# Expert weights in 8 MB units with 16 KB runs and two places, instead of 4 MB units with 8 KB runs and three

## What is computed

```
h = rms_norm(x);  proj = h @ w_in            # q|k|v, RWKV-7 inputs, two gates
attn = sliding_window_attention(q, k, v);  y = rwkv7(...)
merged = sigmoid(ga) * (attn @ w_branch_a) + sigmoid(gb) * (y @ w_branch_b)
x = x + merged @ w_out                       # the output projection, 16 MB of weights
hf = rms_norm(x)
# router: best of 4 groups, best 2 of its 8 experts; for each of 32 experts e:
x[tok] += weight[tok, e] * ((silu(hf[tok] @ w_gate[e]) * (hf[tok] @ w_up[e])) @ w_down[e])
out = rms_norm(x) * final_norm_w
```

## Time and profile before

| | |
|---|---|
| three runs, lowest, median, highest | 1857.42, 1860.07, 1862.98 us |
| the profiled execution, its own time | 1861.89 us |
| its span in the profile | 1860.0 us |
| PE, DVE, ACT busy | 1454.8, 503.5, 347.7 us (78%, 27%, 19%) |
| DMA traffic | 529.04 MB, 284 GB/s over the span |
| chain that ended last | PE 57%, DMA 34%, DVE 4%, ACT 3% |
| mean granted clock of TensorE | 0.89 of full speed |

### The profile page before, as it was taken

How to read it: one execution, slowest core, us unless ns; L and a number is a source line. 1 busy time by engine, 2 the same in 40 slices (tenths; PEclk the granted TensorE clock), 3 DMA queues, 4 the chain that set the end, 5 groups by cost and what they waited for, 6 DMA issues and landing times.

```text
span 1860.0 us, 24062 instructions
## 1 busy us (share of the span) xinstructions
PE 1454.8 (78%) x10818; PEld 834.8 (45%) x10818; DVE 503.5 (27%) x666; ACT 347.7 (19%) x399; POOL 37.3 (2%) x33
## 2 busy tenths in 40 slices
PE   7999999999989999998767567575575665765754
PEld 7999964447546758886312113122121221211311
DVE  5555444252253256644101001010010100100102
ACT  5444332311121134444101001000010000100001
POOL 1000000002001100000000000000000000000000
PEclk9999999899979999999869779788887888977887
DMA  9555424240202239555699999999999999999993
GB/s 355 189 180 181 143 96 147 95 147 21 97 33 76 99 123 331 196 226 203 274 421 422 422 422 422 422 422 422 422 422 421 422 422 421 422 422 421 423 422 146
DMA packets 114524, 529.04 MB, mean 284 GB/s; under 512 B 7408, under 2 KB 9722, under 8 KB 64410
## 3 DMA queue, kind: packets, MB, share of 16 engines
q1 hardware_dynamic: 109616, 514.50, 69.2%
q0 software_dynamic: 2048, 8.24, 1.2%
q10 hardware_dynamic: 2794, 5.31, 0.8%
HBM read 521.74 MB, written 6.29 MB: 284 GB/s over the span
## 4 chain that ended last, share of the span: by engine, by line
PE 57%; DMA 34%; DVE 4%; ACT 3%; issue 1%; ACTq 0%; DVEq 0%; SPq 0%; POOL 0%; POOLq 0%
DMA ring<-in_expert_w_down 17%; DMA ring<-in_expert_w_up 11%; PE ps L508 11%; PE ps L571 10%; PE ps L843 9%; PE ps L961 7%; DMA ring<-in_expert_w_gate 6%; PE ps L978 5%; PE ps L987 3%; PE ps L930 2%; PE ps L470 1%; PE ps L734 1%; PE ps L751 1%; PE ps L553 1%; PE ps L753 1%
## 5 line engine op out<-in xcount | busy, mean ns | idle before, releaser
L961 PE MATMUL ps<-ring,arena 128*32 128x512 f32 x1280 | 184.7, 729 | 99.9 <-DMA ring<-in_expert_w_up 78.7
L571 PE MATMUL ps<-ring,arena 128*128 128x512 f32 x512 | 232.5, 607 | 3.2 <-ACT rs L1141 3.2
L978 PE MATMUL ps<-ring,arena 128*32 128x512 f32 x768 | 129.6, 836 | 85.6 <-DMA ring<-in_expert_w_down 83.5
L961 PE MATMUL ps<-arena 128*32 128x512 f32 x768 | 124.3, 807 | 76.5 <-DMA arena<-in_expert_w_up 46.2
L508 PE MATMUL ps<-h_hi,w_hi 128*128 128x256 f32 x544 | 155.2, 285 | 4.3 <-DVE w_lo L1399 4.3
L508 PE MATMUL ps<-h_lo,w_hi 128*128 128x256 f32 x544 | 155.0, 285 | 0.0
L508 PE MATMUL ps<-h_hi,w_lo 128*128 128x256 f32 x544 | 154.9, 285 | 0.0
L571 PEld LDWEIGHTS ps<-ring,arena 128*128 128x128 f32 x512 | 96.5, 194 | 118.6 <-issue 111.0
L961 PEld LDWEIGHTS ps<-ring,arena 128*32 128x32 f32 x1280 | 47.1, 130 | 223.5 <-issue 128.7
L1799 DVE TENSOR_TENSOR arena<-arena,ps 128x512 f32<-128x512 f32 x64 | 44.0, 688 | 345.1 <-PE ps L987 345.1
L978 PEld LDWEIGHTS ps<-ring,arena 128*32 128x32 f32 x768 | 31.0, 146 | 178.6 <-DMA ring<-in_expert_w_down 87.9
(11 more groups left out here) (292 smaller groups left out, 1798.7 us busy)
## 6 DMA issues: line engine op xcount, KB each, us to landing
ring<-in_expert_w_up SPq DMA_DIRECT2D x24, 4096.0 KB, 25.5
ring<-in_expert_w_down SPq DMA_DIRECT2D x24, 4096.0 KB, 23.9
ring<-in_w_in SPq DMA_DIRECT2D x34, 2048.0 KB, 8.2
arena<-in_expert_w_gate SPq DMA_DIRECT2D x16, 4096.0 KB, 23.7
ring<-in_expert_w_gate SPq DMA_DIRECT2D x16, 4096.0 KB, 23.7
arena<-in_expert_w_up SPq DMA_DIRECT2D x8, 4096.0 KB, 16.5
arena<-in_expert_w_down SPq DMA_DIRECT2D x8, 4096.0 KB, 23.4
ring<-in_w_out SPq DMA_DIRECT2D x8, 2048.0 KB, 7.9
```

Source lines behind the costliest of these rows:

```text
L571: last = mm(ps[:, 7, :], hT[:, k, 128 * t:128 * t + 128], slot(n)[:, k % 8, :], start=k == 0, stop=k == KT - 1)
L961: last = mm(ps[32 * j:32 * j + 32, u % 2, :], XS[:, k, 32 * j:32 * j + 32], w[:, j, kk, :], start=k == 0, stop=k == KT - 1, tile_position= ...
L978: last = mm(ps[32 * j:32 * j + 32, 2 + nb, :], HIDT[:, kh, 32 * j:32 * j + 32], w[:, j, 512 * nb:512 * nb + 512], start=kh == 0, stop=kh == 3,
```

## The change

- A unit is 8 MB: eight blocks of input rows of gate or up for four experts, so that a partition reads 16 KB in one run. A group is six units (gate, up, gate, up, down, down). The down matrices are read with the rows of a partition adjacent, unit 4 in 16 KB runs; unit 5 comes in two parts with runs of 8 KB, each with its own semaphore. The hidden values are transposed with a step of four columns to match.
- There are two places of 8 MB instead of three of 4 MB: even units in arena 0 to 8191 and ring slots 2 and 3, odd units in ring slots 0 and 1 and arena 12288 to 20479. A unit is loaded when the unit two before it is used, in two DMAs of 4 MB (unit 5: four of 2 MB).
- w_out uses ring slots 0 and 1 only: chunk c waits for chunk c-2. Behind the chunks 2 to 5 SyncE issues one quarter (2 MB) each of unit 0. The first half of unit 1 follows when all chunks are used, its second half when TensorE has done its last piece (`v_used` at UM + UO).
- `hfn` moves to arena 8192, over `hfT`, and so ScalarE waits for the logits (`lgT_ps`) before it writes it. `XS`, `YS` and the small tiles move to arena 25344 and up.
- `FW` lies over `XS` now, and GpSimd loads it when unit 3 of the last group is used.
- `gather(3)` runs right behind `gather(2)`, both after unit 0. The second path is adapted; it is left out here.

```diff
--- before.py
+++ after.py
@@ -222,24 +222,25 @@
...
-        hfn = A(12288, 4096).rearrange("p (a d) -> p a d", a=TT)
+        hfn = A(8192, 4096).rearrange("p (a d) -> p a d", a=TT)
         fout = hfn
         hfT = A(8192, 4096).rearrange("p (k t) -> p k t", k=KT)
...
-        junk2 = A(16384, 4096).rearrange("p (a d) -> p a d", a=TT)
+        junk2 = A(12288, 4096).rearrange("p (a d) -> p a d", a=TT)
-        XS = A(16384, 2048).rearrange("p (k s) -> p k s", k=KT)
-        YS = A(18432, 2048)
...
-        FW = A(27648, 2048)
+        XS = A(25344, 2048).rearrange("p (k s) -> p k s", k=KT)
+        YS = A(27392, 2048)
...
+        FW = A(25344, 2048)
@@ -294,7 +295,9 @@

         def v_piece(x):

-            return x // 4, ring[:, x // 4 % RING, 1024 * (x % 4):1024 * (x % 4) + 1024]
+            c = x // 4
+            s = c % RING if x < UM else c % 2
+            return s, ring[:, s, 1024 * (x % 4):1024 * (x % 4) + 1024]
@@ -307,15 +310,22 @@
-        UPG = 12
-        ROWS = 4
-
-        def uslot(u):
-
-            s = u % 3
-            if s == 0:
-                return A(0, 2 * SLOT), S("unit_full0")
-            return ring[:, 2 * s - 2:2 * s, :].rearrange("p a n -> p (a n)"), S(f"unit_full{s}")
+        UPG = 6
+        ROWS = 8
+
+        def place(u, j):
+
+            if u % 2:
+                return ring[:, j, :] if j < 2 else A(12288 + SLOT * (j - 2), SLOT)
+            return A(SLOT * j, SLOT) if j < 2 else ring[:, j, :]
+
+        def pair(u, h):
+
+            if u % 2 == h:
+                first = A(12288 if h else 0, 2 * SLOT)
+                return first.rearrange("p (j n) -> p j n", j=2)
+            return ring[:, 2 * h:2 * h + 2, :]
+
         assert NM % RING == 0 and NO % RING == 0
...
@@ -368,37 +378,54 @@
                     for o, n, key in ((0, 4, "router_group_w"), (4, 32, "router_expert_w")):
                         sp.dma_start(rw[:, :, o:o + n], a[key][0].rearrange("(k p) n -> p k n", p=P)).then_inc(S("rw_in"), 16)
             wo = a["w_out"][0].rearrange("(k p) n -> p k n", p=P)
-            for c in range(8):
-                load(NO + c, slot(NO + c), wo[:, 8 * (c % 2):8 * (c % 2) + 8, 512 * (c // 2):512 * (c // 2) + 512])
-
             eg = a["expert_w_gate"][0].rearrange("e (p k) h -> p e (k h)", p=P)
             eu = a["expert_w_up"][0].rearrange("e (p k) h -> p e (k h)", p=P)
-            ed = a["expert_w_down"][0].rearrange("e (k p) n -> p e k n", p=P)
-
-            def uload(u, first):
-
-                dst, full = uslot(u)
-                if u < 8:
-                    src = (eu if u % 2 else eg)[:, bass.ds(first, GE), ROWS * HID * (u // 2):ROWS * HID * (u // 2 + 1)]
+            ed = a["expert_w_down"][0].rearrange("e (p k) n -> p e (k n)", p=P)
+
+            for c in range(8):
+                sp.wait_ge(S("chunk_used"), NM + 5 + c if c < 2 else NO + c - 1)
+                sp.dma_start(ring[:, c % 2, :].rearrange("p (k n) -> p k n", k=8),
+                             wo[:, 8 * (c % 2):8 * (c % 2) + 8, 512 * (c // 2):512 * (c // 2) + 512])\
+                    .then_inc(S(f"slot_full{c % 2}"), 16)
+                if 2 <= c < 6:
+
+                    if c == 2:
+                        sp.wait_ge(S("v_used"), UM)
+                    if c == 4:
+                        sp.wait_ge(S("chunk_used"), NO)
+                    sp.dma_start(place(0, c - 2), eg[:, c - 2, 0:SLOT]).then_inc(S("unit_full0"), 16)
+
+            def half_unit(u, h, first):
+
+                src = (eu if u % 2 else eg) if u < 4 else ed
+                sp.dma_start(pair(u, h), src[:, bass.ds(first, 2), SLOT * (u // 2 % 2):SLOT * (u // 2 % 2) + SLOT])\
+                    .then_inc(S(f"unit_full{u % 2}"), 16)
+
+            def uload(u, firsts):
+
+                if u < UPG - 1:
+                    for h in range(2):
+                        half_unit(u, h, firsts[h])
                 else:
-                    src = ed[:, bass.ds(first, GE), u - 8, :]
-                sp.dma_start(dst.rearrange("p (j n) -> p j n", j=GE), src).then_inc(full, 16)
-
-
-            sp.wait_ge(S("v_used"), UM)
-            uload(0, 0)
-            sp.wait_ge(S("chunk_used"), NE - 2)
-            uload(1, 0)
+
+                    for r in range(2):
+                        for h in range(2):
+                            sp.dma_start(pair(u, h)[:, :, 2048 * r:2048 * r + 2048],
+                                         ed[:, bass.ds(firsts[h], 2), SLOT + 2048 * r:SLOT + 2048 * r + 2048])\
+                                .then_inc(S(("unit_full1", "unit_last")[r]), 16)
+
             sp.wait_ge(S("chunk_used"), NE)
-            uload(2, 0)
-            for u in range(3, UPG):
-                sp.wait_ge(S("unit_used"), u - 2)
-                uload(u, 0)
+            half_unit(1, 0, 0)
+            sp.wait_ge(S("v_used"), UM + UO)
+            half_unit(1, 1, 2)
+            for u in range(2, UPG):
+                sp.wait_ge(S("unit_used"), u - 1)
+                uload(u, (0, 2))
             with sp.Fori(1, GROUPS) as g:
-                first = sp.snap(g * GE)
+                firsts = (sp.snap(g * GE), sp.snap(g * GE + 2))
                 for u in range(UPG):
-                    sp.wait_ge(S("unit_used"), g * UPG + (u - 2))
-                    uload(u, first)
+                    sp.wait_ge(S("unit_used"), g * UPG + (u - 1))
+                    uload(u, firsts)
@@ -457,6 +483,8 @@
+            pool.wait_ge(S("unit_used"), UPG * GROUPS - 2)
+            pool.dma_start(FW, a["final_norm_w"].partition_broadcast(P)).then_inc(S("fw_in"), 16)
@@ -938,47 +966,48 @@
                 gather(1, g * 7 + 1)

                 pe.wait_ge(S("hid_done"), g + 1)
-                for u in range(8):
-                    if u == 2:
-
-                        pe.wait_ge(S("b0_free"), g * 7 + 2)
+                for u in range(4):
+                    pe.wait_ge(S(f"unit_full{u % 2}"), g * 96 + 32 * (u // 2 + (1 if u % 2 else 2)))
+                    for kk in range(ROWS):
+                        k = ROWS * (u // 2) + kk
+                        if u % 2 == 0 and kk % 4 == 0:
+
+                            q = k // 4
+                            pe.wait_ge(S(f"b{q % 2}_free"), g * 7 + (2, 2, 4, 3)[q])
+                        for j in range(GE):
+                            last = mm(ps[32 * j:32 * j + 32, u % 2, :], XS[:, k, 32 * j:32 * j + 32],
+                                      place(u, j)[:, HID * kk:HID * kk + HID],
+                                      start=k == 0, stop=k == KT - 1, tile_position=(0, 32 * j))
+                    last.then_inc(S("unit_used"), 1)
+                    if u == 0:
+
                         pe.wait_ge(S("ohw_done"), g + 1)
                         for t in range(TT):
                             last = tp(ps[:, 6, 128 * t:128 * t + 128], OHW[:, 128 * t:128 * t + 128])
                         last.then_inc(S("b0_full"), 1)
                         gather(2, g * 7 + 3)
-                    if u == 4:
                         gather(3, g * 7 + 2)
-                    if u % 2 == 0:
-
-                        pe.wait_ge(S(f"b{u // 2 % 2}_free"), g * 7 + (2, 2, 4, 3)[u // 2])
-                    w, sem = uslot(u)
-                    pe.wait_ge(sem, g * 64 + 16 * (u // 3 + 1))
-                    w = w.rearrange("p (j k h) -> p j k h", j=GE, k=ROWS)
-                    for kk in range(ROWS):
-                        k = ROWS * (u // 2) + kk
-                        for j in range(GE):
-                            last = mm(ps[32 * j:32 * j + 32, u % 2, :], XS[:, k, 32 * j:32 * j + 32], w[:, j, kk, :],
-                                      start=k == 0, stop=k == KT - 1, tile_position=(0, 32 * j))
-                    last.then_inc(S("unit_used"), 1)
                 pe.wait_ge(S("hid_done"), g + 2)
                 pe.wait_ge(S("flag_set"), 1)
                 for k in range(4):
-                    last = tp(ps[:, 7, 128 * k:128 * k + 128], HIDB[:, 128 * k:128 * k + 128])
+                    last = tp(ps[:, 7, 128 * k:128 * k + 128], HIDB.rearrange("s (m k) -> s k m", k=4)[:, k, :])
                 last.then_inc(S("b1_full"), 1)

                 pe.wait_ge(S("b1_free"), g * 7 + 4)
                 pe.wait_ge(S("ys_done"), g + 1)
                 for kh in range(4):
-                    w, sem = uslot(8 + kh)
-                    pe.wait_ge(sem, g * 64 + 16 * ((8 + kh) // 3 + 1))
-                    w = w.rearrange("p (j n) -> p j n", j=GE)
+                    u, r = 4 + kh // 2, kh % 2
+                    if kh == 0:
+                        pe.wait_ge(S("unit_full0"), g * 96 + 32 * 4)
+                    elif kh > 1:
+                        pe.wait_ge(*((S("unit_last"), g * 32 + 32) if r else (S("unit_full1"), g * 96 + 32 * 3)))
                     for nb in range(4):
                         for j in range(GE):
                             last = mm(ps[32 * j:32 * j + 32, 2 + nb, :], HIDT[:, kh, 32 * j:32 * j + 32],
```

(67 more changed lines are left out.)

## The result

The changed kernel takes 1847.84 us (median of 4 runs, 1846.31 to 1848.58), the kernel before 1860.39 in the same comparison (4 runs). The ratio is 0.9929, with a 95% interval of 0.9913 to 0.9945: faster by 12.6 us (0.7%), between 10 and 16. The forecast was 1846.3, from -13.8 us. The profiled execution of the changed kernel took 1846.31 us, with a span of 1844.4.

A forecast was written before the change was run, and what follows sets the result against it. The expert stage was taken as a byte stream: start + 3.8 + bytes/rate + 33.4. Terms -9.9 + 5.0 - 11.4 + 2.5 = -13.8 us gave 1848.1 for the profiled execution, 1846.3 us for the median; range 1840 to 1860.

The forecast's parts named there:

- step 1: Expert stream: 16 MB instead of 12 MB loaded ahead, so one 4 MB load less in the stream, -9.9 us.
- step 2: Stream start: first place free only after 8 MB (3.4 us), ScalarE waiting for the logits (1.6 us), +5.0 us.
- step 3: Expert stream: 16 KB runs save 9.4 ns per joined pair of packets, -11.4 us.
- The three cycles per packet: Contrary skill figure for the long runs in the stream: 3.5 ns per packet, saving an estimated 4.3 us, median 1853.4.
- The instruction loads' 1.08 us a packet: Rival reading for the stream: 16 KB packets are slow in themselves, costing hundreds of us; chance 0.02.
- step 4: End of the stream: FW's 1 MB load moves inside it, +2.5 us.
- step 5: w_out stage: chunks through two slots still land in time, costing nothing, by 3.4 us.
- the rival: w_out stage: a quarter going ahead of the next chunk makes five chunks 1.4 us late, +7 us; chance 0.06.
- step 6: Group borders in the stream: two places instead of three cost nothing, by 7.5 us.
- the slower rival: Group borders: PE late at two places, queue runs dry, 5.1 us at each of seven borders, 1882; chance 0.08.
- Tail: From the last part's first product to the span's end: unchanged at 33.4 us.

The follow-up runs named there:

- The short runs: Changed kernel, but units 0 to 4 of each group come in four DMAs of 2 MB with 8 KB runs: 1857.64 us (ratio 0.9984).
- The run with three more rounds: Changed kernel with gathers 0 and 1 done three more times in every group, results overwritten: 1870.39 us (ratio 1.0047).
- The run that was to show the wait for the logits: Kernel before, with ScalarE waiting for the logits before it writes the normalised tokens: 1863.12 us (ratio 1.0011).

## Why the prediction was right

- **Bytes (step 1).** -9.9 forecast; the run that puts 4 MB back into the stream lost 9.9 by the medians and 10.4 by the profile's stream.
- **Start (step 2).** +5.0 forecast, +5.9 measured in the profiled execution, and that it came so near is in part luck. Unit 0 as the first whole place gave 3.44 us, against 3.4. The wait for the logits gave 1.43, against 1.6, but only because this execution ran the logits at a low clock (3.16 us at a mean of 0.57). I read the 3.42 us of the kernel before as their fixed length; at the full clock they take 1.89, and the wait is then worth 0.17, in the kernel before too. The remaining 1.06 us are a term that I had at nothing: the first gathers take 6.30 us instead of 5.24, at a mean granted clock of 0.59 instead of 0.72, behind a longer pause of PE (3.90 us, 2.27 before). An execution with the logits at the full clock starts its stream at 38.6, 4.7 later than the profile before.
- **Runs (step 3).** -11.4 forecast. The short runs gave 9.8 back by the medians and 11.4 by the profile's stream, 1.52 us a group, 9.5 ns a packet. The straight line through 2 KB and 8 KB held at 16 KB. The three cycles per packet of the Trainium skill (DMA: Bandwidth & Descriptors, "Why small descriptors are slow (HBM only)") would have been an estimated 0.6 us a group; the trace disagrees, and the measurement decides. The ceiling that the Trainium skill gives on the same page, in the section "Where 436 GB/s comes from", is 435 GB/s; whole groups reach 427, below it. The instruction loads' 1.08 us a packet was, as argued, not the price of 16 KB.
- **FW (step 4).** +2.5 forecast; 120.20 - 117.77 = 2.4 in the changed kernel, and 2.6 gained when it moved out.
- **Two slots for w_out (step 5).** Nothing, as forecast; 128.46 us from chunk 0's issue to the last release, and nothing even when a quarter goes first, which the rival had priced at +7 us.
- **Two places (step 6).** Nothing, as forecast, but the term was mis-sized. I took all of the 3.8 us from issue to first product as the lead that a refill needs. The run with three more rounds shows 2.4; the rest must lie behind the last byte, where the steady stream pays it too (argued, not shown). So the border's slack is 8.5 us, not 7.5, and the slower rival was further away than I priced it: a refill at T + 38.1 would lose some 1.4 us a border, as the one at T + 38.0 lost 1.1, not 2.8.
- **Tail.** 33.4 forecast, 32.0 measured: L1016 was 1.5 us shorter than L987 had been. That is the clock again (1.00 and 0.81), and luck.

The sum is right within its terms' errors: by the profile, without the first line of the table, -14.3 against -13.8; by the medians -12.6, whose interval holds both. The stream, on which the argument rests, is 0.1 us off (909.22 against 909.3). The start is 0.9 us too long and the tail 1.4 too short, and these two cancel in part by chance.

## What to carry to other kernels

When a stage is a saturated stream, write its time as start + bytes/rate + tail and price an edit by the term that it moves; here the length of the contiguous runs (9.5 ns for each packet saved) and 4 MB more loaded ahead gave about -11 and -10 us, and a load put into the stream cost its bytes. Two large places fed the queue as well as three small ones here, with each refill issued at least 2.4 us before the queue was empty; measure that slack by adding work until the period moves. Read changes of under 1% from periods and fixed points in the profile, since the medians carry the wander of stages that nobody touched. And before you take a wait's length from one profile, look at the clock of the products that it waits for: here the same eight took 1.89 or 3.42 us, and the same wait was worth 0.17 or 1.4 us.

## What was not expected

- An idle queue costs 3.8 us from issue to first product (903.19 to 926.68 for 8 MB at 9.8 us per half), but a refill has to be issued only 2.4 us before the queue is empty for the stream to lose nothing.
- The DMA rate in the stream does not depend on how the same bytes are cut into DMAs: 4 MB or 2 MB each, the group is 117.77 or 117.76 us.
- The changed kernel is insensitive to PE work at its borders: +3.8 us per group moved its period by nothing. The kernel before is less so: the same work made its periods 0.2 to 1.7 us longer. It would have been more had L995 not taken 7.72 us instead of 9.39 at most borders, so that part of the added work was given back by PE's own speed.
- The run that was to show the wait for the logits returned the forecast number, 1.55 us against 1.6, for another reason: 1.38 of it were slower gathers.
